# Expert weights against interleaved tokens: stationary blocks laid out in rows of 62 and 30 words

## Chip, cores and metric

The kernel runs on one core of one Trainium2 chip. The metric is the device time of one execution in microseconds. Everything is computed in float32 values. A float32 product is made from rounded parts (float32r): each operand is split into a high part and the low rest, and three matmuls of parts are summed.

## The reference, cut to what matters

Two layers of a streaming encoder run over 256 prompt tokens and 64 sample tokens, 1024 features wide. The change concerns the last stage alone, the top-2-of-8 SwiGLU experts of the second layer:

```python
def moe_ffn(x, w_r, wg, wu, wd):
    ...
    for e in range(N_EXPERTS):          # 8
        h = jax.nn.silu(xt @ wg[e]) * (xt @ wu[e])        # 1024 -> 3584
        y = y + gates[:, e:e + 1] * jnp.dot(h, wd[e])     # 3584 -> 1024
```

## The kernel before

The first 576 us compute both mixers and the dense feed-forward. What follows is the expert stage. Each expert works on a block of up to 128 tokens that were sent to it, gathered as rows into `xg`.

The weights of one expert come in 42 pieces (`NP`) of 128 x 2048 words, 336 pieces in all: 28 pieces of gate and up weights, 14 of down weights. SyncE loads a piece into one of seven slots of `raw` (L648). ScalarE rounds it into `split_hi` (`piece_hi`, L1207), and VectorE writes the rest, `raw - split_hi`, into `split_lo` (`piece_lo`, L1808). Both have three slots (`SR`), and ScalarE waits for TensorE to have used the piece three before.

On TensorE the weights are the moving operand, 512 columns at a time, and the tokens are the stationary one. A stationary operand is 128 partitions (features) by 128 columns (tokens), and each matmul loads its own. There are four sets of such blocks: `xgT_hi` and `xgT_lo` with 8 blocks each (the normalised input, transposed), and `hmT_hi` and `hmT_lo` with 28 blocks each (the gated hidden rows, transposed). For each piece TensorE issues 12 matmuls: high tokens and low tokens by high weights, then high tokens by low weights. They are L2475, L2479, L2484 for gate and up, L2510, L2513, L2519 for down, and L2495, L2496, L2502 for the last down piece:

```python
for c, o in enumerate(outs):
    TE.matmul(o, xgT_hi[:, kk, :], hi[:, w * k + 512 * c:w * k + 512 * c + 512], start=kk == 0, stop=False)
...
```

How the blocks are made: `hm` is transposed on TensorE by four transposes into one PSUM bank (L2528), in which the transposed tile is the stationary operand and takes every fourth word:

```python
last = TE.transpose(tb[n % 2][:, 128 * k:128 * k + 128], hm[:, m % 2, k:512:4], ident)
```

ScalarE copies the bank into `hmT_hi` with rounding (L1303), VectorE writes the rest to `hmT_lo` (L1952). This happens seven times for each expert. Near the end of an expert (piece `X_AT` = 39) the next expert's rows, which TensorE has transposed from `xg` by eight transposes (L1984), are scaled and written to `xgT_hi` by ScalarE (`xg_hi`, L1255) and to `xgT_lo` by VectorE (`xg_lo`, L1823).

At the very end the last expert's result is split into `last_y_hi` and `last_y_lo`, which lie in the places of `xgT_hi` and `xgT_lo`, and is sent back to its tokens by six matmuls for each of two halves (L2544 to L2552). In these every third one has a stationary operand of 64 columns.

The order of the work is written out by hand on each engine, and semaphores join the engines. Nothing of that order is changed.

Of the kernel before, what the change touches and what calls it, by code (L numbers as in the profile page):

```python
# [16 lines left out]
F32 = mybir.dt.float32  # L17
# [8 lines left out]
P = 128  # L26
D = 1024
# [221 lines left out]
def build(nc, A, O):  # L249
# [5 lines left out]
    with ExitStack() as ctx:  # L255
# [163 lines left out]
        hmT_hi = sb("hmT_hi", [P, FEB, P], FR)  # L419
# [38 lines left out]
        xgT_hi = sb("xgT_hi", [P, KB, P], FR)  # L458
        xgT_lo = sb("xgT_lo", [P, KB, P], FR)
# [5 lines left out]
        sb("below_hmT_lo", [P, 384])  # L465
        loop_only = ExitStack()
        hmT_lo = sb("hmT_lo", [P, FEB, P], FR, loop_only)
# [98 lines left out]
        last_y_hi = xgT_hi[:].rearrange("p k n -> p (k n)")  # L566
        last_y_lo = xgT_lo[:].rearrange("p k n -> p (k n)")
# [316 lines left out]
        def _(act):  # L884
# [364 lines left out]
            def xg_hi(base, first, ks=range(KB)):  # L1249

                for k in ks:
# [3 lines left out]
                    last = nc.scalar.activation(xgT_hi[:, k, :], b[:, 128 * (k % 4):128 * (k % 4) + 128], ACT.Copy, scale=gcol(3)[:, k:k + 1])  # L1255
# [18 lines left out]
            def experts(count, ip, done):  # L1274

                for i in range(done, count * NP):
# [51 lines left out]
        def _(dve):  # L1328
# [488 lines left out]
            def xg_lo(first, base, ks=range(KB)):  # L1817

                for k in ks:
                    if k % 4 == 0:  # L1820
                        dve.wait_ge(th_ready, base + (first + k // 4 + 1))
                    b = tb[(first + k // 4) % 2]
                    last = V.scalar_tensor_tensor(out=xgT_lo[:, k, :], in0=b[:, 128 * (k % 4):128 * (k % 4) + 128], scalar=gcol(3)[:, k:k + 1],  # L1823
                                                  in1=xgT_hi[:, k, :].bitcast(F32), op0=ALU.mult, op1=ALU.subtract)
# [103 lines left out]
            def experts(count, ip, done):  # L1928

                for i in range(done, count * NP):  # L1930
# [17 lines left out]
                    if q in HT_AT:  # L1948
# [3 lines left out]
                        V.tensor_tensor(hmT_lo[:, 4 * j:4 * j + 4, :].rearrange("p b n -> p (b n)"), tb[n % 2][:],  # L1952
                                        hmT_hi[:, 4 * j:4 * j + 4, :].rearrange("p b n -> p (b n)").bitcast(F32), ALU.subtract).then_inc(t_free, 1)
# [22 lines left out]
        def _(pe):  # L1976
# [462 lines left out]
            def experts(count, ip, first=False):  # L2439

                for i in range(count * NP):
# [27 lines left out]
                    if j < 2 * FC:  # L2469
                        n, w = 4 // len(ms), 512 * len(ms)  # L2470
                        outs = [banks[2 * up + (FC * h + m) % 2][:] for m in ms]
                        for k in range(n):
                            kk = n * s + k
                            for c, o in enumerate(outs):
                                TE.matmul(o, xgT_hi[:, kk, :], hi[:, w * k + 512 * c:w * k + 512 * c + 512], start=kk == 0, stop=False)  # L2475
                            if first and i == 0:
                                continue
                            for c, o in enumerate(outs):
                                TE.matmul(o, xgT_lo[:, kk, :], hi[:, w * k + 512 * c:w * k + 512 * c + 512], start=False, stop=False)  # L2479
                        pe.wait_ge(lo_ready, ip * (2 * NP) + (i + 1 + PR))  # L2480
                        for k in range(n):
                            kk = n * s + k
                            for c, o in enumerate(outs):
                                last = TE.matmul(o, xgT_hi[:, kk, :], lo[:, w * k + 512 * c:w * k + 512 * c + 512], start=False, stop=kk == KB - 1)  # L2484
# [122 lines left out]
```

## Time and profile before

| | us |
|---|---|
| median of 3 runs | 1537.97 |
| lowest and highest run | 1537.42, 1539.92 |
| span of the profiled execution, first to last instruction | 1535.8 |
| TensorE matmul busy | 1527.8 |
| TensorE weight load busy | 1333.0 |
| VectorE busy | 1234.4 |
| ScalarE busy | 998.9 |
| GpSimd busy | 217.5 |

The profiled execution has no time of its own beside its span, so sums are made on the span. The weight load is a queue of its own beside the matmuls and overlaps them. The record of a matmul is longer than its distance to the next one, since matmuls are pipelined: 390 ns long at a distance of 227 ns. The distance of their starts is what a matmul costs; in the merged timeline it is found from the starts of two lines and the counts between them.

### The profile page before, as it was taken

To read this page: it belongs to the slowest core of one execution; us is meant where nothing else is said; L and a number is where in the kernel's file an instruction comes from. 1 tells how busy PE (TensorE), PEld (TensorE's weight loads), DVE (VectorE), ACT (ScalarE), POOL (GpSimd) and SP (SyncE) were. 2 spreads that over 40 slices of the span, in tenths; PEclk is the share of its full clock that TensorE was granted. 3 is DMA by queue.
4 is the path that set the end of the run, shared out by engine and by line. 5 is a ranking of instruction groups with operands and counts; after the bars stand their busy time and mean duration, and the time that the engine had idled before them with its cause. 6 is when DMAs were issued, how large, how long until landed. Compare 5 with 4: busy or idle time off the path is not lost.

```text
span 1535.8 us, 21611 instructions
## 1 busy us (share of the span) xinstructions
PE 1527.8 (99%) x8428; PEld 1333.0 (87%) x8428; DVE 1234.4 (80%) x1253; ACT 998.9 (65%) x1079; POOL 217.5 (14%) x249
## 2 busy tenths in 40 slices
PE   9999999999999999999999999999999999999998
PEld 7989999999998988888888888888888888888887
DVE  5877666654477758988988888998998988898897
ACT  5655433333466547777777778777777777777775
POOL 5514400001150403101001001002002002002000
PEclk9999999999999999999999999999999999999999
DMA  8333455444443459999999999999999999999994
GB/s 226 96 110 116 149 164 164 133 157 151 125 122 110 141 209 367 383 366 388 372 381 376 374 374 376 391 359 386 384 363 382 381 362 379 400 361 363 394 373 183
DMA packets 159701, 437.43 MB, mean 285 GB/s; under 512 B 12068, under 2 KB 66176, under 8 KB 145264
## 3 DMA queue, kind: packets, MB, share of 16 engines
q1 hardware_dynamic: 151796, 423.02, 75.0%
q0 software_dynamic: 5552, 9.62, 2.3%
q10 hardware_dynamic: 2252, 3.41, 0.7%
q8 instruction: 68, 1.11, 0.3%
q14 instruction: 33, 0.27, 0.1%
HBM read 429.40 MB, written 13.60 MB: 288 GB/s over the span
## 4 chain that ended last, share of the span: by engine, by line
PE 98%; DMA 0%; ACT 0%; DVE 0%; issue 0%; SPq 0%; DVEq 0%; ACTq 0%
PE bank L1981 34%; PE bank L2475 13%; PE bank L2484 13%; PE bank L2479 13%; PE bank L2510 6%; PE bank L2513 6%; PE bank L2519 6%; PE bank L1984 3%; PE bank L2528 2%; PE bank L2496 0%; PE bank L2502 0%; PE bank L2495 0%; DMA gla<-b_g 0%; DVE x L1972 0%; ACT L1076 0%
## 5 line engine op out<-in xcount | busy, mean ns | idle before, releaser
L1808 DVE TENSOR_TENSOR split_lo<-raw,split_hi 128x2048 fp32r<-128x2048 f32 x336 | 763.1, 2289 | 101.8 <-ACT split_hi L1207 100.8
L1207 ACT CAST split_hi<-raw 128x2048 fp32r<-128x2048 f32 x336 | 640.5, 1911 | 224.5 <-PE bank L2484 145.7
L2475 PE MATMUL bank<-split_hi,xgT_hi 128*128 128x512 f32 x896 | 291.7, 395 | 0.0
L2479 PE MATMUL bank<-split_hi,xgT_lo 128*128 128x512 f32 x892 | 285.8, 390 | 0.0
L2484 PE MATMUL bank<-split_lo,xgT_hi 128*128 128x512 f32 x896 | 239.9, 390 | 0.0
L913 ACT CAST cut_hi<-ring 128x1024 fp32r<-128x1024 f32 x124 | 129.9, 1048 | 166.6 <-PE bank L1981 166.6
L1981 PE MATMUL bank<-xT_hi,cut_hi 128*128 128x320 f32 x752 | 236.7, 315 | 0.0
L1981 PE MATMUL bank<-xT_hi,cut_lo 128*128 128x320 f32 x752 | 233.5, 310 | 0.0
L1981 PE MATMUL bank<-xT_lo,cut_hi 128*128 128x320 f32 x752 | 231.9, 308 | 0.0
L1346 DVE TENSOR_TENSOR cut_lo<-ring,cut_hi 128x1024 fp32r<-128x1024 f32 x124 | 153.0, 1235 | 80.7 <-ACT cut_hi L913 79.9
L2484 PEld LDWEIGHTS bank<-split_lo,xgT_hi 128*128 128x128 f32 x896 | 168.3, 188 | 34.9
L2479 PEld LDWEIGHTS bank<-split_hi,xgT_lo 128*128 128x128 f32 x892 | 167.7, 188 | 34.7
L2475 PEld LDWEIGHTS bank<-split_hi,xgT_hi 128*128 128x128 f32 x896 | 166.2, 189 | 32.3
L1981 PEld LDWEIGHTS bank<-xT_hi,cut_hi 128*128 128x128 f32 x752 | 142.1, 189 | 1.6
L1981 PEld LDWEIGHTS bank<-xT_lo,cut_hi 128*128 128x128 f32 x752 | 142.2, 189 | 0.0
L1981 PEld LDWEIGHTS bank<-xT_hi,cut_lo 128*128 128x128 f32 x752 | 142.0, 189 | 0.0
L2510 PE MATMUL bank<-split_hi,hmT_hi 128*128 128x512 f32 x416 | 129.8, 393 | 0.0
L2513 PE MATMUL bank<-split_hi,hmT_lo 128*128 128x512 f32 x416 | 128.3, 390 | 0.0
L2519 PE MATMUL bank<-split_lo,hmT_hi 128*128 128x512 f32 x416 | 111.3, 390 | 0.0
L853 POOL COPY idc<-idx 128x1 uint32 (+1 forms) x8 | 5.7, 707 | 635.9 <-PE bank L1984 616.0
L2513 PEld LDWEIGHTS bank<-split_hi,hmT_lo 128*128 128x128 f32 x416 | 78.2, 188 | 16.3
L2519 PEld LDWEIGHTS bank<-split_lo,hmT_hi 128*128 128x128 f32 x416 | 78.1, 188 | 16.2
(316 smaller groups left out, 1723.2 us busy)
## 6 DMA issues: line engine op xcount, KB each, us to landing
raw<-moe_w_gate SPq DMA_DIRECT2D x112, 1024.0 KB, 7.8
raw<-moe_w_up SPq DMA_DIRECT2D x112, 1024.0 KB, 7.6
raw<-moe_w_down SPq DMA_DIRECT2D x112, 1024.0 KB, 7.3
ring<-w_in SPq DMA_DIRECT2D x15, 1024.0 KB, 5.5
ring<-ffn_w_gate SPq DMA_DIRECT2D x11, 1024.0 KB, 5.5
ring<-ffn_w_up SPq DMA_DIRECT2D x11, 1024.0 KB, 5.4
ring<-ffn_w_down SPq DMA_DIRECT2D x10, 1024.0 KB, 5.1
ring<-w_out SPq DMA_DIRECT2D x8, 1024.0 KB, 5.0
```

Source lines behind the costliest of these rows:

```text
L913: nc.scalar.copy(split_cut(cut_hi, q), raw_cut(q)).then_inc(cut_hi_ready, 1)
L1207: return nc.scalar.copy(split_hi[:, i % SR, :], raw_piece(i)).then_inc(hi_ready, 1)
L1346: V.tensor_tensor(split_cut(cut_lo, q), raw_cut(q), split_cut(cut_hi, q).bitcast(F32), ALU.subtract).then_inc(cut_lo_ready, 1)
L1808: V.tensor_tensor(split_lo[:, i % SR, :], raw_piece(i), split_hi[:, i % SR, :].bitcast(F32), ALU.subtract).then_inc(lo_ready, 1)
L1981: return TE.matmul(out, lhsT, rhs, start=start, stop=stop)
L1984: return TE.transpose(out, in_, ident[0:rows, 0:rows])
L2475: TE.matmul(o, xgT_hi[:, kk, :], hi[:, w * k + 512 * c:w * k + 512 * c + 512], start=kk == 0, stop=False)
L2479: TE.matmul(o, xgT_lo[:, kk, :], hi[:, w * k + 512 * c:w * k + 512 * c + 512], start=False, stop=False)
L2484: last = TE.matmul(o, xgT_hi[:, kk, :], lo[:, w * k + 512 * c:w * k + 512 * c + 512], start=False, stop=kk == KB - 1)
L2510: TE.matmul(banks[6 + n][:], hmT_hi[:, b, :], hi[:, c], start=b == 0, stop=False)
L2513: TE.matmul(banks[6 + n][:], hmT_lo[:, b, :], hi[:, c], start=False, stop=False)
L2519: last = TE.matmul(banks[6 + n][:], hmT_hi[:, b, :], lo[:, c], start=False, stop=b == FEB - 1)
```

## The change

The 128 words of one stationary block no longer lie side by side. In the new tile `spread` each token has a row of 62 words: words 0 to 7 are `xgT_hi`, 8 to 15 `xgT_lo`, 16 to 43 `hmT_lo`, and the rest is unused. In `spread_hi` each token has a row of 30 words, of which 28 are `hmT_hi`. So the consecutive columns of a stationary operand lie 248 or 120 bytes apart. The writes of ScalarE and VectorE go to the same places, one word every 248 or 120 bytes, and VectorE reads `hmT_hi` and `xgT_hi` back so. `last_y` gets a contiguous tile of its own where `xgT_hi` and `xgT_lo` were. Small pads place the two tiles 128 bytes further on than they would be without them; the tiles that lie above `spread_hi` move by 1,280 bytes, and `spread` by 1,152.

```diff
-        hmT_hi = sb("hmT_hi", [P, FEB, P], FR)
+        sb("below_spread_hi", [P, 32])
+        spread_hi = sb("spread_hi", [P, P, 30], FR)
+        sb("above_spread_hi", [P, 32])
...
-        xgT_hi = sb("xgT_hi", [P, KB, P], FR)
-        xgT_lo = sb("xgT_lo", [P, KB, P], FR)
+        last_y = sb("last_y", [P, 2, D], FR)
...
-        sb("below_hmT_lo", [P, 384])
+        sb("below_spread", [P, 352])
         loop_only = ExitStack()
-        hmT_lo = sb("hmT_lo", [P, FEB, P], FR, loop_only)
+        spread = sb("spread", [P, P, 62], FR, loop_only)
...
+        last_y_hi, last_y_lo = last_y[:, 0], last_y[:, 1]
+
+        def xgT_hi(k):
+            return spread[:, :, 0 + k]
+
+        def xgT_lo(k):
+            return spread[:, :, 8 + k]
+
+        def hmT_hi(b):
+            return spread_hi[:, :, 0 + b]
+
+        def hmT_lo(b):
+            return spread[:, :, 16 + b]
+
+        HMT_HI, HMT_LO = (spread_hi, 0), (spread, 16)
+
+        def four(part, j):
+            tile, first = part
+            return tile[:, :, first + 4 * j:first + 4 * j + 4].rearrange("p n s -> p s n")
+
+        def four_in(bank):
+            return bank[:].rearrange("p (s n) -> p s n", s=4)
...
-                    last = nc.scalar.activation(xgT_hi[:, k, :], b[:, 128 * (k % 4):128 * (k % 4) + 128], ACT.Copy, scale=gcol(3)[:, k:k + 1])
+                    last = nc.scalar.activation(xgT_hi(k), b[:, 128 * (k % 4):128 * (k % 4) + 128], ACT.Copy, scale=gcol(3)[:, k:k + 1])
...
-                        nc.scalar.copy(hmT_hi[:, 4 * j:4 * j + 4, :].rearrange("p b n -> p (b n)"), tb[n % 2][:]).then_inc(th_ready, 1)
+                        nc.scalar.copy(four(HMT_HI, j), four_in(tb[n % 2])).then_inc(th_ready, 1)
...
-                        V.tensor_tensor(hmT_lo[:, 4 * j:4 * j + 4, :].rearrange("p b n -> p (b n)"), tb[n % 2][:],
-                                        hmT_hi[:, 4 * j:4 * j + 4, :].rearrange("p b n -> p (b n)").bitcast(F32), ALU.subtract).then_inc(t_free, 1)
+                        V.tensor_tensor(four(HMT_LO, j), four_in(tb[n % 2]), four(HMT_HI, j).bitcast(F32), ALU.subtract).then_inc(t_free, 1)
...
-                                TE.matmul(o, xgT_hi[:, kk, :], hi[:, w * k + 512 * c:w * k + 512 * c + 512], start=kk == 0, stop=False)
+                                TE.matmul(o, xgT_hi(kk), hi[:, w * k + 512 * c:w * k + 512 * c + 512], start=kk == 0, stop=False)
```

The other matmuls of the stage and `xg_lo` change in the same way.

## Rows read from the trace of the kernel before

**Rows 1.** The page: span, rate of transfers in 40 slices, chain that ended last.
```profile
span 1535.8 us, 21611 instructions
...
GB/s 226 96 110 116 149 164 164 133 157 151 125 122 110 141 209 367 383 366 388 372 381 376 374 374 376 391 359 386 384 363 382 381 362 379 400 361 363 394 373 183
...
PE bank L1981 34%; PE bank L2475 13%; PE bank L2484 13%; PE bank L2479 13%; PE bank L2510 6%; PE bank L2513 6%; PE bank L2519 6%; PE bank L1984 3%; PE bank L2528 2%; PE bank L2496 0%; PE bank L2502 0%; PE bank L2495 0%; DMA gla<-b_g 0%; DVE x L1972 0%; ACT L1076 0%
```

**Rows 2.** Views of xgT_hi and hmT_hi: min/median/max ns, first and last start.
```profile
L2475 PE MATMUL bank<-split_hi,xgT_hi x896: 387/390/508, 576.5 to 1486.8; 128*128 128x512 f32 x180
...
L2510 PE MATMUL bank<-split_hi,hmT_hi x416: 388/390/477, 657.0 to 1523.3; 128*128 128x512 f32 x139
...
L2495 PE MATMUL bank<-split_hi,hmT_hi x32: 388/390/390, 693.8 to 1526.7; 128*128 128x512 f32 x32
...
L2502 PE MATMUL bank<-split_lo,hmT_hi x32: 389/390/390, 694.7 to 1527.4; 128*128 128x512 f32 x32
```

**Rows 3.** Timeline of TensorE at the tail: start us, us, instructions merged.
```profile
1527.65 0.85 PE L2544 MATMUL bank<-xgT_hi,last_hot 128*128 128x512 f32 x3
1528.33 0.84 PE L2548 MATMUL bank<-xgT_lo,last_hot 128*128 128x512 f32 x3
1529.01 0.86 PE L2544 MATMUL bank<-xgT_hi,last_hot 128*128 128x512 f32 x3
```

**Rows 4.** One stretch: length, PE, PEld, DVE, ACT, POOL busy, clock, DMA.
```profile
700.00:800.00 100.00, 100.00 (x459) 83.45 (x458) 89.06 (x50) 75.39 (x50) 5.39 (x4) 1.00 1.01 382
```

**Rows 5.** Timeline of TensorE around four transposes of hm.
```profile
720.10 1.07 PE L2484 MATMUL bank<-split_lo,xgT_hi 128*128 128x512 f32 x4
...
722.82 1.08 PE L2484 MATMUL bank<-split_lo,xgT_hi 128*128 128x512 f32 x4
723.74 0.63 PE L2528 MATMUL bank<-const_sb,hm 128*128 128x128 f32 x4
...
724.67 0.62 PE L2479 MATMUL bank<-split_hi,xgT_lo 128*128 128x512 f32 x2
```

**Rows 6.** Timeline of TensorE around eight transposes of xg.
```profile
678.41 1.07 PE L2519 MATMUL bank<-split_lo,hmT_hi 128*128 128x512 f32 x4
679.32 1.03 PE L1984 MATMUL bank<-const_sb,xg 128*128 128x128 f32 x8
...
680.66 0.62 PE L2513 MATMUL bank<-split_hi,hmT_lo 128*128 128x512 f32 x2
```

**Rows 7.** Weight loads (tile views: min/median/max ns; by line: busy us, mean ns).
```profile
L2544 PEld LDWEIGHTS bank<-xgT_hi,last_hot x6: 134/188/188, 1527.4 to 1529.2; 128*128 128x128 f32 x4, 128*64 128x64 f32 x2
...
L2528 PEld LDWEIGHTS bank<-const_sb,hm 128*128 128x128 f32 x224 | 35.6, 204 | 4.5 <-DVE hm L1946 0.5
...
L1984 PEld LDWEIGHTS bank<-const_sb,xg 128*128 128x128 f32 x64 | 7.5, 140 | 1.0
...
L2528 PE MATMUL bank<-const_sb,hm x224: 270/283/386, 604.7 to 1499.4; 128*128 128x128 f32 x112
```

**Rows 8.** VectorE's splits of 2048 and 1024 elements: busy us, mean ns, idle before.
```profile
L1808 DVE TENSOR_TENSOR split_lo<-raw,split_hi 128x2048 fp32r<-128x2048 f32 x336 | 763.1, 2289 | 101.8 <-ACT split_hi L1207 100.8
...
L1346 DVE TENSOR_TENSOR cut_lo<-ring,cut_hi 128x1024 fp32r<-128x1024 f32 x124 | 153.0, 1235 | 80.7 <-ACT cut_hi L913 79.9
```

**Rows 9.** Timeline of VectorE at the end of the first expert.
```profile
687.33 2.15 DVE L1823 SCALAR_TENSOR_TENSOR xgT_lo<-bank,pcol,xgT_hi 128x128 fp32r<-128x128 f32 x8
689.40 8.90 DVE L1808 TENSOR_TENSOR split_lo<-raw,split_hi 128x2048 fp32r<-128x2048 f32 x4
```

**Rows 10.** Timeline of TensorE: sixteen fp32 matmuls with eight stationary columns.
```profile
560.77 4.47 PE L1981 MATMUL bank<-xR,wr 128*8 128x320 f32 x16
```

**Rows 11.** The same by line from 559 to 566 us: busy us, mean ns.
```profile
L1981 PE MATMUL bank<-xR,wr 128*8 128x320 f32 x16 | 4.5, 433 | 0.0
```

**Rows 12.** Timeline of TensorE in the dense feed-forward, 18 matmuls apart.
```profile
400.06 0.31 PE L1981 MATMUL bank<-hT_hi,cut_hi 128*128 128x320 f32 x1
...
402.70 0.31 PE L1981 MATMUL bank<-hT_hi,cut_hi 128*128 128x320 f32 x1
```

More of the change, by code:

```diff
@@ L1822, in xg_lo @@
                     b = tb[(first + k // 4) % 2]
-                    last = V.scalar_tensor_tensor(out=xgT_lo[:, k, :], in0=b[:, 128 * (k % 4):128 * (k % 4) + 128], scalar=gcol(3)[:, k:k + 1],
-                                                  in1=xgT_hi[:, k, :].bitcast(F32), op0=ALU.mult, op1=ALU.subtract)
+                    last = V.scalar_tensor_tensor(out=xgT_lo(k), in0=b[:, 128 * (k % 4):128 * (k % 4) + 128], scalar=gcol(3)[:, k:k + 1],
+                                                  in1=xgT_hi(k).bitcast(F32), op0=ALU.mult, op1=ALU.subtract)
                     if k % 4 == 3:
@@ L2478, in experts @@
                             for c, o in enumerate(outs):
-                                TE.matmul(o, xgT_lo[:, kk, :], hi[:, w * k + 512 * c:w * k + 512 * c + 512], start=False, stop=False)
+                                TE.matmul(o, xgT_lo(kk), hi[:, w * k + 512 * c:w * k + 512 * c + 512], start=False, stop=False)
                         pe.wait_ge(lo_ready, ip * (2 * NP) + (i + 1 + PR))
@@ L2483, in experts @@
                             for c, o in enumerate(outs):
-                                last = TE.matmul(o, xgT_hi[:, kk, :], lo[:, w * k + 512 * c:w * k + 512 * c + 512], start=False, stop=kk == KB - 1)
+                                last = TE.matmul(o, xgT_hi(kk), lo[:, w * k + 512 * c:w * k + 512 * c + 512], start=False, stop=kk == KB - 1)
                         if first and i == 0:
@@ L2488, in experts @@
                                 for c, o in enumerate(outs):
-                                    last = TE.matmul(o, xgT_lo[:, k, :], hi[:, w * k + 512 * c:w * k + 512 * c + 512], start=False, stop=False)
+                                    last = TE.matmul(o, xgT_lo(k), hi[:, w * k + 512 * c:w * k + 512 * c + 512], start=False, stop=False)
                     elif q == NP - 1:
@@ L2494, in experts @@
                                 c = slice(1024 * k + 512 * n, 1024 * k + 512 * n + 512)
-                                TE.matmul(banks[6 + n][:], hmT_hi[:, b, :], hi[:, c], start=False, stop=False)
-                                TE.matmul(banks[6 + n][:], hmT_lo[:, b, :], hi[:, c], start=False, stop=False)
+                                TE.matmul(banks[6 + n][:], hmT_hi(b), hi[:, c], start=False, stop=False)
+                                TE.matmul(banks[6 + n][:], hmT_lo(b), hi[:, c], start=False, stop=False)
                             if n == 0:
@@ L2501, in experts @@
                                 c = slice(1024 * k + 512 * n, 1024 * k + 512 * n + 512)
-                                last = TE.matmul(banks[6 + n][:], hmT_hi[:, b, :], lo[:, c], start=False, stop=k == 1)
+                                last = TE.matmul(banks[6 + n][:], hmT_hi(b), lo[:, c], start=False, stop=k == 1)
                             if n == 0:
@@ L2518, in experts @@
                                 c = slice(1024 * k + 512 * n, 1024 * k + 512 * n + 512)
-                                last = TE.matmul(banks[6 + n][:], hmT_hi[:, b, :], lo[:, c], start=False, stop=b == FEB - 1)
+                                last = TE.matmul(banks[6 + n][:], hmT_hi(b), lo[:, c], start=False, stop=b == FEB - 1)
                     last.then_inc(piece_used, 1)
```

6 lines of the change are left out of this document (2 added, 4 removed).

## Prediction

> **What bounds the kernel now.** I read the page first. Its span is 1535.8 us [rows 1]; the median of the runs shown, 1537.97 us, lies 2.2 us above it, and I add those 2.2 us to every sum made on this execution. The experts' matmuls run from 576.5 us [rows 2] to 1527.65 us [rows 3], 951 us. Inside it TensorE is busy for all of a 100 us window while VectorE is at 89% and ScalarE at 75% [rows 4]. The chain that ended last goes through TensorE's lines only: L2475, L2484 and L2479 with 13% each, L2510 and L2513 with 6% each [rows 1]. So the question is what one expert matmul costs TensorE from start to start, not how long its record is.
>
> The timeline gives that. Between the starts of the last four matmuls of one piece and of the next piece, 720.10 and 722.82, lie 12 matmuls: 2.72 us, 0.2267 us each [rows 5]. At 2.4 GHz (granted clock 1.00 [rows 4]) 512 columns take 0.2133, so 13.4 ns per matmul are not columns. The count is 896 on L2475, 416 on L2510, 32 on L2495 [rows 2], each with two companions: 4032 matmuls, 914 us. The rest are transposes. From 722.82 to 724.67 stand six such matmuls and four transposes of `hm`: 1.85 less 1.36 is 0.49 us for four [rows 5]; from 678.41 to 680.66 six matmuls and eight transposes of `xg`: 2.25 less 1.36 is 0.89 for eight [rows 6]. With 56 fours and 8 eights that is 914 + 27 + 7 = 948 of the 951 us. There is no stall to win back; the stage is 4032 cadences.
>
> **What the change moves.** (a) No instruction is added or removed. Every one of the 4032 stationary operands, until now 128 consecutive words, becomes 128 words that lie 248 or 120 bytes apart. (b) ScalarE and VectorE write these words, and VectorE reads the high ones back, at the same distance. (c) Tiles above lie 1,280 or so bytes further on.
>
> **(a) on the path.** A load of weights runs beside the matmul before it. For contiguous fp32r weights it takes 188 ns with 128 columns and 134 with 64 [rows 7]: 0.84 ns a column on top of 80 ns. The 0.84 × 128 = 108 ns of columns have a cadence of 227 ns to hide in. What does distance cost? The trace has one distant stationary: `hm[:, m % 2, k:512:4]`, one word in 16 bytes. Its load takes 204 ns, that of the contiguous `xg` in the same kind of transpose 140 [rows 7]. Less the 80 ns, 0.97 against 0.47 ns a column: twice as slow. Transposes of `xg` cost 0.89/8 = 0.111 us each, those of `hm` 0.49/4 = 0.122, so where the load is the limit the distance shows.
>
> It matters here only if the load outgrows 227 ns, or disturbs the stream of the matmul beside it. For the first: if a distant column costs 0.97 ns in an fp32r load too, the load is 80 + 0.97 × 128 = 204 ns long, with 124 ns of columns: hidden. For the second: the first `hm` load of a group runs beside an fp32r matmul. The last four matmuls before `hm` start at 722.82, and the first `hm` transpose at 723.74: 0.92 us [rows 5]; before `xg` 678.41 to 679.32, 0.91 [rows 6]. One resolution step apart, so a distant load beside a 512-column stream costs at most 0.01 us in this one place, and the nearest row gives nothing. I take nothing for (a): the cover is the 213 ns stream, and the price without it is in the first rival. Ends kept: a gain of 11 ns and a loss of 17 ns per matmul, from the rivals.
>
> [...]
>
> **(b) off the path.** VectorE takes (2289 - 1235)/1024 = 1.03 ns an element [rows 8]; I use it for ScalarE too. No row writes at such a distance; below nothing I see no reason for a gain, above I allow a doubling, as for the load. Then each `hmT` copy grows by 512 elements, 0.53 us, seven times an expert, and the eight `xgT` pieces by 1.05 us together, on either engine. VectorE gets 4.8 us more in an expert's 118.6 us (948.5/8) and goes from 89% to 93%: no bound. The tightest place is the end of an expert. There the eight `xgT` low parts take 2.15 us and four piece splits follow without a break, 8.90 us; the second ends at 693.85 [rows 9], and the matmul that reads it, the first of L2502, starts at 694.7 [rows 2]: 0.85 us to spare. I take nothing for (b); with both doublings 2.1 us would arrive there, 1.25 beyond the cover.
>
> **(c)** The same 0.2267 holds over `xgT` and `hmT` and all three slots of the split tiles, so I price placement at nothing. `last_y` stays contiguous, and the tail is unchanged. The DMA queue moves the same bytes.
>
> Sum: 1535.8 + 0 + 0 + 0, and 2.2: 1538.0 us. Its own range is 1535 to 1541.
>
> **Rivals.** *A load that pays twice (slower).* A contiguous fp32r load takes 0.84 ns a column where the transpose's takes 0.47. If that is because it goes over its columns twice, a distant column costs 2 × 0.97 = 1.94 ns, and 248 ns of columns no longer fit under 227. Twice the cadence of load-bound `hm` transposes is 2 × 0.122 = 0.244 us; taken from inside a group, (0.63 - 0.283)/3 = 0.116 [rows 5], where 0.283 is the length of one record [rows 7], it is 0.231. The cost is 4032 × 5 to 17 ns, 20 to 70 us; in the middle 45, 1583 us. It decides as soon as a column costs above 227/128 = 1.77 ns. [...] Chance 0.20. [...]
>
> *The 13.4 ns are a collision between the load's reads and the stream's, and the new distance avoids it (faster).* An fp32 matmul of 320 columns beside a load of eight columns has a cadence of (4.47 - 0.43)/15 = 0.269 us [rows 10, 11], two passes of 133.3 ns and only 2.7 ns over. So without a full load beside it a matmul can follow at 2 to 3 ns. The full prize is 11 ns × 4032 = 44 us: 1494 us. VectorE's 2.51 us a piece (89% of 948.5/336) fits under the 2.69 that would be left, and the transfers would have to go from 382 [rows 4] to about 400 GB/s, where single slices show 400 [rows 1]. Against it: 18 matmuls of 320 columns take 402.70 - 400.06 = 2.64 us, 0.1467 each, 13.4 ns over 133.3 [rows 12]: the excess does not grow with the stream. At the tail every third load has 64 columns instead of 128, and six matmuls take 1.36 us, 0.2267 each [rows 3], no less than elsewhere as far as rows of 10 ns can tell: it doesn't shrink with the load either. A fixed cost per switch would not care about layout. But all of these loads are contiguous; the trace has no fp32r matmul beside a distant fp32r load, and 13 ns could be the part of many collisions that any contiguous walk has. It pays from 0.8 ns a matmul. Chance 0.33.
>
> *Distant writes that come late (slower, small).* As worked out under (b): 1.25 us at eight places, 10 us, 1548. It decides once both engines' additions exceed 0.85 us. Nothing shows the price of such writes. Chance 0.10.
>
> **How the numbers follow.** Forecast 0.37, the three rivals 0.33, 0.20 and 0.10. The prediction is the likeliest case, 1538 us. A change under 0.2% (3 us) can't be told from none here. Faster is the collision case, 0.33; same 0.37; slower 0.20 + 0.10 = 0.30. As cases of both signs hold most of the chance, the range has to reach both full prices: from 1493 to 1585 us; more than the middle of the slow case is the part left out.
>
> **What would show it.** If I am right, in the profile after the loads of L2475 to L2519 have a mean of about 204 ns instead of 188, and a piece still takes 2.72 us. The twice-paying load shows a load record near 330 ns and a piece of 2.8 to 2.9 us. The collision shows a piece near 2.6 us, with load records of any length. Late writes show as ScalarE's and VectorE's `spread` rows growing, and a gap in front of L2502. I am wrong above all if an fp32r load reads otherwise than a transpose's does, since the one distant load of this trace is a transpose's.

## The result, and the profile after

| | before | after |
|---|---|---|
| median (lowest to highest), us | 1537.93 (1537.42 to 1539.92), 4 runs | 1619.31 (1617.7 to 1620.85), 4 runs |
| ratio, 95% interval | | 1.0532, 1.0517 to 1.0547 |
| span of the profiled execution, us | 1535.8 | 1619.1 |

The change costs 81.4 us. That is 5.3%, on the slow side and beyond the range that ended at 1585. Divided by the 4032 matmuls it is 20.2 ns each.

The page of the changed kernel answers to [rows 1]: the span, the busy times, the rate of transfers and the chain.
```profile
span 1619.1 us, 21611 instructions
...
PE 1610.3 (99%) x8428; PEld 1572.8 (97%) x8428; DVE 1274.7 (79%) x1253; ACT 1033.8 (64%) x1079; POOL 216.9 (13%) x249
...
GB/s 215 93 129 124 153 157 150 145 161 131 118 136 91 170 344 359 337 353 351 343 338 363 342 331 371 341 330 368 342 345 360 336 335 362 344 344 333 364 337 164
...
PE 98%; DMA 0%; ACT 0%; DVE 0%; issue 0%; SPq 0%; DVEq 0%; ACTq 0%
```
The number of instructions is the same. A slice is now 40.5 us long instead of 38.4, so the expert stage begins in the 15th; from the 16th slice on each one moves less per second than before. The time went into the expert stage, and TensorE is still the whole chain. What is new is the weight load (PEld): it was busy for 1333.0 of 1535.8 us, and is now for 1572.8 of 1619.1.

The weight loads by line and shape, changed kernel (busy us, mean ns, idle before); [rows 7] had 188 ns for a load of this shape:
```profile
L2499 PEld LDWEIGHTS bank<-split_hi,spread 128*128 128x128 f32 x892 | 264.0, 334 | 0.0
L2495 PEld LDWEIGHTS bank<-split_hi,spread 128*128 128x128 f32 x896 | 263.9, 332 | 0.1
...
L2539 PEld LDWEIGHTS bank<-split_lo,spread_hi 128*128 128x128 f32 x416 | 112.4, 335 | 0.0
L2548 PEld LDWEIGHTS bank<-const_sb,hm 128*128 128x128 f32 x224 | 35.8, 204 | 0.9
```
"Distant" means here and below that neighbouring words of a block don't lie side by side. In these rows the distant fp32r loads take 332 to 335 ns (328 to 335 over all lines of the stage), and the queue has next to no idle time before them. The distant transposes of `hm`, which the change does not touch, still take 204.

Busy time of each engine, granted clock and transfers between 700 and 800 us of the changed kernel, as in [rows 4]:
```profile
700.00:800.00 100.00, 100.00 (x418) 99.91 (x418) 86.79 (x48) 73.64 (x49) 4.88 (x3) 1.00 0.97 352
```
The clock is still 1.00, so it is not the clock. VectorE went from 89.06 to 86.79 although its writes grew: it now works for a slower TensorE, with 48 operations in the window instead of 50. The loads fill 99.91 of 100 us, and 418 instead of 459 matmuls fit.

The timeline of TensorE in the changed kernel, around one group of transposes and at the same place of two pieces four apart, as in [rows 5]:
```profile
736.42 1.14 PE L2504 MATMUL bank<-split_lo,spread 128*128 128x512 f32 x4
737.40 0.63 PE L2548 MATMUL bank<-const_sb,hm 128*128 128x128 f32 x4
737.79 0.84 PE L2495 MATMUL bank<-split_hi,spread 128*128 128x512 f32 x2
738.47 0.66 PE L2499 MATMUL bank<-split_hi,spread 128*128 128x512 f32 x2
...
747.41 0.65 PE L2495 MATMUL bank<-split_hi,spread 128*128 128x512 f32 x2
...
759.20 0.65 PE L2495 MATMUL bank<-split_hi,spread 128*128 128x512 f32 x2
```
From 747.41 to 759.20 are 48 matmuls, 0.2456 us each, where it was 0.2267. That is 18.9 ns, and 4032 of them are 76.2 us. From 736.42 to 738.47 are six matmuls and four transposes: 2.05 us, less 6 × 0.2456 leaves 0.576 for the four, where 0.49 was left. The first two matmuls behind the transposes take 0.68 us, where two take 0.49 elsewhere. The likely reason is that the load behind the last short transpose has no 213 ns stream to hide under. (The 213 ns are 512 columns at 0.4167 ns: 512 columns take 0.2267 us [rows 5] and 320 take 0.1467 [rows 12], 0.0800 us for 192 more. The prediction's 2.4 GHz comes to the same 0.4167.) 56 × 0.086 is 4.8 us. The two together are 81.0 of the 81.4 us: carried over to the whole stage, these distances account for the loss.

The copies into the distant tiles, changed kernel (min/median/max ns, first and last start):
```profile
L1324 ACT CAST spread_hi<-bank x56: 1159/1177/1197, 614.0 to 1585.3; 128x512 fp32r<-128x512 f32 x56
L1973 DVE TENSOR_TENSOR spread<-bank,spread_hi x56: 1150/1208/1251, 616.3 to 1587.6; 128x512 fp32r<-128x512 f32 x56
```
In the kernel before these two took 577 and 684 ns (medians of L1303 and L1952). ScalarE's copy doubled (2.04 times), VectorE's took 1.77 times as long. The prediction had allowed 0.53 us more for each; they are 0.60 and 0.52.

VectorE at the end of the first expert in the changed kernel, as in [rows 9]:
```profile
697.57 3.06 DVE L1844 SCALAR_TENSOR_TENSOR spread<-bank,pcol,spread 128x128 fp32r<-128x128 f32 x8
700.53 8.98 DVE L1829 TENSOR_TENSOR split_lo<-raw,split_hi 128x2048 fp32r<-128x2048 f32 x4
...
705.98 0.65 PE L2522 MATMUL bank<-split_lo,spread_hi 128*128 128x512 f32 x2
```
The last line is TensorE's, from its timeline. The eight low parts take 3.06 instead of 2.15 us. The second split behind them ends near 705.0 (700.53 + half of 8.98), and its reader starts at 705.98. Nothing waits here: the cover is 0.95 us, where it was 0.85.

### The profile page after: what moved, and what is told of

Same layout as the page of the kernel before. It is cut to its first block, busy times and chain, and to the rows that moved or that the text cites. A ratio compares the mean times of both kernels' runs of the same rounds, so it can differ in the third digit from the quotient of the medians.

```text
span 1619.1 us, 21611 instructions
## 1 busy us (share of the span) xinstructions
PE 1610.3 (99%) x8428; PEld 1572.8 (97%) x8428; DVE 1274.7 (79%) x1253; ACT 1033.8 (64%) x1079; POOL 216.9 (13%) x249
## 4 chain that ended last, share of the span: by engine, by line
PE 98%; DMA 0%; ACT 0%; DVE 0%; issue 0%; SPq 0%; DVEq 0%; ACTq 0%
PE bank L2001 32%; PE bank L2495 14%; PE bank L2504 14%; PE bank L2499 14%; PE bank L2530 6%; PE bank L2539 6%; PE bank L2533 6%; PE bank L2004 3%; PE bank L2548 2%; PE bank L2516 0%; PE bank L2522 0%; PE bank L2515 0%; DMA gla<-b_g 0%; DVE x L1992 0%; ACT L1097 0%
## 5 line engine op out<-in xcount | busy, mean ns | idle before, releaser
L2495 PE MATMUL bank<-split_hi,spread 128*128 128x512 f32 x896 | 311.8, 418 | 0.0
L2499 PE MATMUL bank<-split_hi,spread 128*128 128x512 f32 x892 | 302.1, 408 | 0.0
L2495 PEld LDWEIGHTS bank<-split_hi,spread 128*128 128x128 f32 x896 | 263.9, 332 | 0.1
L2499 PEld LDWEIGHTS bank<-split_hi,spread 128*128 128x128 f32 x892 | 264.0, 334 | 0.0
L2504 PE MATMUL bank<-split_lo,spread 128*128 128x512 f32 x896 | 256.9, 409 | 0.0
L2504 PEld LDWEIGHTS bank<-split_lo,spread 128*128 128x128 f32 x896 | 239.8, 334 | 0.0
L2001 PE MATMUL bank<-xT_hi,cut_hi 128*128 128x320 f32 x752 | 236.5, 314 | 0.0
L2530 PE MATMUL bank<-split_hi,spread_hi 128*128 128x512 f32 x416 | 139.4, 416 | 0.0
L2533 PE MATMUL bank<-split_hi,spread 128*128 128x512 f32 x416 | 136.2, 409 | 0.0
L2530 PEld LDWEIGHTS bank<-split_hi,spread_hi 128*128 128x128 f32 x416 | 121.0, 335 | 0.0
L2539 PE MATMUL bank<-split_lo,spread_hi 128*128 128x512 f32 x416 | 120.2, 411 | 0.0
L2533 PEld LDWEIGHTS bank<-split_hi,spread 128*128 128x128 f32 x416 | 119.5, 330 | 0.0
L2539 PEld LDWEIGHTS bank<-split_lo,spread_hi 128*128 128x128 f32 x416 | 112.4, 335 | 0.0
```

Source lines behind the costliest of these rows:

```text
L2001: return TE.matmul(out, lhsT, rhs, start=start, stop=stop)
L2495: TE.matmul(o, xgT_hi(kk), hi[:, w * k + 512 * c:w * k + 512 * c + 512], start=kk == 0, stop=False)
L2499: TE.matmul(o, xgT_lo(kk), hi[:, w * k + 512 * c:w * k + 512 * c + 512], start=False, stop=False)
L2504: last = TE.matmul(o, xgT_hi(kk), lo[:, w * k + 512 * c:w * k + 512 * c + 512], start=False, stop=kk == KB - 1)
L2530: TE.matmul(banks[6 + n][:], hmT_hi(b), hi[:, c], start=b == 0, stop=False)
L2533: TE.matmul(banks[6 + n][:], hmT_lo(b), hi[:, c], start=False, stop=False)
```

## The experiments

All ratios are against the kernel before. "Cadence" is the distance of two starts of the timeline divided by the matmuls between them, in gate and up pieces past 1000 us where not said otherwise. The theories at the start, by the letters that the expectations use: the load reads a distant word at about twice the price and no longer fits under the stream (L); a distant load slows the stream beside it (S); the distant writes come late or get in TensorE's way (W). A fourth is the place of the tiles.

### Writes and reads apart

**Distant writes, contiguous reads.** All of the changed kernel's writes stay. TensorE reads one contiguous block instead, a copy of the identity:
```diff
+        still = sb("still", [P, P], FR)
...
+            V.tensor_copy(still[:], ident).then_inc(still_ready, 1)
...
-                                TE.matmul(o, xgT_hi(kk), hi[:, w * k + 512 * c:w * k + 512 * c + 512], start=kk == 0, stop=False)
+                                TE.matmul(o, still[:], hi[:, w * k + 512 * c:w * k + 512 * c + 512], start=kk == 0, stop=False)
```


> The changed kernel, but all 4032 expert matmuls take one contiguous stationary block of 128 words (the identity) instead of the distant ones, so the experts' products are left out; ScalarE and VectorE still write and read back every distant word. Theory L (the weight load itself reads distant words at about 1.95 ns a column and sets the cadence): loads back at 188 ns, a piece 2.72 us, 1538 to 1542 us. Theory S (a distant load disturbs the stream beside it): the same. Theory W (ScalarE's and VectorE's distant accesses come late or compete with TensorE's reads): the 81 us stay, about 1619 us.

Measured: 1544.72 us against 1536.07, ratio 1.0054 (1.0037 to 1.0071). The loads, a stretch of the stage, and the timeline at its start in this kernel:
```profile
L2507 PEld LDWEIGHTS bank<-split_lo,still 128*128 128x128 f32 x896 | 168.7, 188 | 35.3
```
```profile
578.15 2.08 PE L2498 MATMUL bank<-split_hi,still 128*128 128x512 f32 x4 [3.35 <-DVE still L1899]
...
583.34 0.62 PE L2498 MATMUL bank<-split_hi,still 128*128 128x512 f32 x2
...
1000.26 1.07 PE L2507 MATMUL bank<-split_lo,still 128*128 128x512 f32 x4
...
1011.14 1.07 PE L2507 MATMUL bank<-split_lo,still 128*128 128x512 f32 x4
```
```profile
578.00:583.00 5.00, 4.85 (x11) 3.80 (x12) 3.58 (x28) 1.49 (x2) 2.14 (x3) 0.50 1.02 365
```
The loads are back at 188 ns and the cadence at 10.88/48 = 0.2267 us. What is left over is mostly the experiment's own. TensorE waits 3.35 us for the copy of the identity and starts the stage at 578.15 us instead of 576.46. The twelve matmuls that follow run at a granted clock of 0.50: (583.34 - 578.15)/12 is 0.4325 us instead of 0.2267, 2.5 us in all. An expert lasts 119.0 us instead of 118.73, which is 2.2 us over eight. These three are 6.4 of the 6.5 us between the two spans, and only the 2.2 can be charged to distant writes. W falls as the cause of the 81 us.

The 2.2 us are real, though, and lie where the prediction looked for them. The loads of the last low parts of an expert, VectorE's timeline before them, and TensorE's at that place:
```profile
L2525 PEld LDWEIGHTS bank<-split_lo,still 128*128 128x128 f32 x32 | 5.4, 188 | 3.5 <-DVE split_lo L1831 2.8
```
```profile
694.79 8.90 DVE L1831 TENSOR_TENSOR split_lo<-raw,split_hi 128x2048 fp32r<-128x2048 f32 x4
```
```profile
699.01 0.39 PE L2519 MATMUL bank<-split_hi,still 128*128 128x512 f32 x1
699.34 0.73 PE L2525 MATMUL bank<-split_lo,still 128*128 128x512 f32 x2
```
The second of the four splits ends near 694.79 + 4.45 = 699.24, and its reader starts at 699.34, 0.33 us behind the matmul before it instead of 0.227. The cover of 0.85 us is used up, and TensorE waits there once in each of the eight experts.

**Distant reads, contiguous writes.** The kernel before, except that every matmul of the stage reads one block at 120 bytes a column:
```diff
+        still = sb("still", [P, P, 30], FR)
...
+            V.tensor_copy(still[:, :, 0], ident).then_inc(still_ready, 1)
...
-                                TE.matmul(o, xgT_hi[:, kk, :], hi[:, w * k + 512 * c:w * k + 512 * c + 512], start=kk == 0, stop=False)
+                                TE.matmul(o, still[:, :, 0], hi[:, w * k + 512 * c:w * k + 512 * c + 512], start=kk == 0, stop=False)
```


> The kernel before, with all its writes contiguous, but all 4032 expert matmuls take one stationary block whose 128 words lie 120 bytes apart (the identity), so the experts' products are left out. L and S: load records near 332 ns, a piece 2.96 us, 1615 to 1622 us. W: 1538 us. Together with the distant writes alone the two differences should add up to the 81 us.

Measured: 1636.18 us, ratio 1.0645 (1.0627 to 1.0663). One of its rows of loads, and the start and end of three pieces of its timeline:
```profile
L2487 PEld LDWEIGHTS bank<-split_lo,still 128*128 128x128 f32 x896 | 243.5, 339 | 0.4
```
```profile
1011.08 1.16 PE L2487 MATMUL bank<-split_lo,still 128*128 128x512 f32 x4
...
1020.06 1.16 PE L2487 MATMUL bank<-split_lo,still 128*128 128x512 f32 x4
```
Reads alone give the loss, and more: the cadence is 8.98/36 = 0.2494 us, not 0.2456, and the 100 us exceed the 81. Some 5.7 us are the late start, as above (the stage begins at 580.59 us, and its first eight matmuls, at a mean granted clock of 0.52, take (584.18 - 580.59)/8 = 0.449 us each), 91.5 are the cadence, which leaves some 3 for the transposes. So the 1615 to 1622 us that were expected, and the two differences adding up to 81, did not come. In this kernel every block lies at 120 bytes, and all matmuls read the same one; at 120 bytes alone the series below has 0.2475 us. The other 2 ns are not explained.

### Is the load the limit?

**Fewer moving columns.** The changed kernel with 384 of the 512 moving columns in all but the first matmul of a sum:
```diff
-                                TE.matmul(o, xgT_lo(kk), hi[:, w * k + 512 * c:w * k + 512 * c + 512], start=False, stop=False)
+                                TE.matmul(o[:, 0:N], xgT_lo(kk), hi[:, w * k + 512 * c:w * k + 512 * c + N], start=False, stop=False)
```


> The changed kernel with 384 instead of 512 moving columns in every expert matmul but the first of each sum; a quarter of the experts' outputs is left out. L: the load needs its 247 ns however short the stream is, so the cadence stays at 0.247 us and the time within 3 us of 1619. S: the stream costs 160 + 13 + 20 = 193 ns, TensorE is no longer the bound, VectorE's work of some 113 us an expert is, about 1490 us.

Measured: 1613.63 us, ratio 1.0497 (1.0479 to 1.0514). Five pieces of its timeline:
```profile
1001.93 1.15 PE L2505 MATMUL bank<-split_lo,spread 128*128 128x384 f32 x4
...
1016.66 1.14 PE L2505 MATMUL bank<-split_lo,spread 128*128 128x384 f32 x4
```
14.73/60 is 0.2455 us. A quarter of the stream is gone, 128 × 0.4167 = 53 ns a matmul, and the cadence is the same as far as rows of 10 ns tell. In the changed kernel the load is the limit, not the stream. S, which expected 0.193 us, falls as the cause of the loss. The time is 5.7 us below the changed kernel's, a little outside the 3 us that L allowed: over a whole expert it is 128.29 us instead of 128.99, or 1.4 ns for each of 504 matmuls. So the shorter stream gives back a little, but not more.

**Fewer stationary columns.** The changed kernel with 96 of 128 stationary columns in nearly all matmuls:
```diff
-                                TE.matmul(o, xgT_lo(kk), hi[:, w * k + 512 * c:w * k + 512 * c + 512], start=False, stop=False)
+                                TE.matmul(o[0:M_], xgT_lo(kk)[:, 0:M_], hi[:, w * k + 512 * c:w * k + 512 * c + 512], start=False, stop=False)
```


> The changed kernel with 96 instead of 128 stationary columns in every expert matmul but the first and last of each sum; 32 of an expert's tokens are left out of most sums. L: the load's columns take 96 x 1.97 = 189 ns (record 270) and hide under 227, so the cadence is 0.227 again, except for about 32 of 504 matmuls: 1541 to 1547 us. S: three quarters of the 20 ns stay, about 1599 us. It also tells whether the cost has a threshold or grows with every column.

Measured: 1571.76 us, ratio 1.0226 (1.0209 to 1.0244). A row of its loads, and two pieces of its timeline in which every load has 96 columns:
```profile
L2500 PEld LDWEIGHTS bank<-split_hi,spread 128*96 128x96 f32 x892 | 222.4, 260 | 0.0
```
```profile
1009.11 1.10 PE L2505 MATMUL bank<-split_lo,spread 128*96 128x512 f32 x4
...
1014.72 1.09 PE L2505 MATMUL bank<-split_lo,spread 128*96 128x512 f32 x4
```
The load gets 74 ns shorter for 32 columns. Its 260 - 80 = 180 ns of columns now fit under the stream, but the cadence is 5.61/24 = 0.2338 us and not 0.2267. Neither expected time came, 1541 to 1547 (L) or 1599 (S). So there is a second cost, 7.1 ns here, that remains when the load is hidden, and L has only the first of the two.

### The price against the distance

Here only `xgT` changes, 2688 of the 4032 matmuls (L2475, L2479, L2484), in the kernel before; `hmT` stays contiguous and serves as a control. One token's row is of r words. For 2, 3, 4 and 16 words the 16 blocks lie in groups of r, for the others in one:
```diff
-        xgT_hi = sb("xgT_hi", [P, KB, P], FR)
-        xgT_lo = sb("xgT_lo", [P, KB, P], FR)
+        xrows = sb("xrows", [P, 4, P, 4], FR)
...
+        def xgT_hi(k):
+            return xrows[:, k // 4, :, k % 4]
```
8 bytes, rows of 2 words:

> [...] If any distance other than one word costs the full price: 332 ns and 1592 us.

12 bytes, rows of 3 words:

> [...] By full price for any distance: 1592.

16 bytes, rows of 4 words, where the changed kernel has the far distances of 120 and 248 bytes:

> [...] If the far distance has a price of its own (banks): less than 1592.

64 bytes, rows of 16 words:

> The same with rows of 16 words: columns 64 bytes apart, in the same 8 KB of the tile as before. [...] If banks that repeat every 64 or 128 bytes matter: clearly more than at 16 bytes.

128 bytes, rows of 32 words:

> The kernel before with only xgT_hi and xgT_lo (2688 matmuls) in rows of 32 words, columns 128 bytes apart. [...] Theory B (memory banks repeat every 128 bytes, and a load whose next column falls into the same bank waits for it; 120 and 248 bytes are 8 short of such a period, so every second step stays in the bank): every step stays in the bank, record well over 339 ns, cadence over 0.250 us.

72 bytes, rows of 18 words:

> [...] Theory B: no step stays in the bank, record 302 to 312 ns, cadence 0.236.

120 bytes, rows of 30 words:

> The kernel before with only xgT_hi and xgT_lo (2688 matmuls) in rows of 30 words, 120 bytes apart, as spread_hi has them. Theory C (the distance of 120 bytes itself makes the load slow): record 333 to 340 ns, cadence 0.246 to 0.250 us, an expert of about 125.5 us. Theory D (placement, or that every block is distant, made it slow): record 302 to 312, cadence 0.236, as at 16, 64, 72 and 128 bytes.

124 bytes, rows of 31 words:

> The same in rows of 31 words, 124 bytes apart, 4 short of 128. If the load gets slow the nearer the distance comes to 128 bytes from below: record at least 335 ns. If 120 bytes is special by itself: 302 to 312.

136 bytes, rows of 34 words:

> The same in rows of 34 words, 136 bytes apart, 8 over 128. If it is the sign that counts, a walk that falls behind the 128-byte period while the stream runs forward: record 302 to 312 ns. If it is the two steps within one 16-byte column of the period, forward or back: about 335 ns.

| distance, bytes | us (before) | ratio, interval | load record, ns | cadence, ns |
|---|---|---|---|---|
| 8 | 1553.83 (1535.99) | 1.0115, 1.0098 to 1.0132 | 193 | 233.3 |
| 12 | 1561.80 (1535.99) | 1.0169, 1.0152 to 1.0186 | 253 | 235.5 |
| 16 | 1564.00 (1535.99) | 1.0186, 1.0169 to 1.0203 | 312 | 236.7 |
| 64 | 1566.18 (1535.99) | 1.0199, 1.0182 to 1.0216 | 302 | 236.5 |
| 72 | 1564.49 (1537.3) | one run | 306 | 235.6 |
| 128 | 1570.27 (1537.3) | one run | 305 | 237.4 |
| 120 | 1598.20 (1535.29) | one run | 334 | 247.5 |
| 124 | 1574.38 (1535.29) | one run | 315 | 239.6 |
| 136 | 1594.78 (1535.29) | one run | 332 | 246.7 |

A row of loads of the kernel with 8 bytes, and its control:
```profile
L2490 PEld LDWEIGHTS bank<-split_lo,xrows 128*128 128x128 f32 x896 | 173.3, 193 | 36.1
...
L2519 PEld LDWEIGHTS bank<-split_hi,hmT_lo 128*128 128x128 f32 x416 | 78.1, 188 | 16.4
```
Five pieces of the timeline at 8 bytes (14.00/60 = 0.2333):
```profile
999.78 1.09 PE L2490 MATMUL bank<-split_lo,xrows 128*128 128x512 f32 x4
...
1013.78 1.10 PE L2490 MATMUL bank<-split_lo,xrows 128*128 128x512 f32 x4
```
A row of loads of the kernel with 16 bytes:
```profile
L2485 PEld LDWEIGHTS bank<-split_hi,xrows 128*128 128x128 f32 x892 | 249.7, 312 | 0.0
```
And with 120, with two pieces of its timeline (5.94/24 = 0.2475):
```profile
L2485 PEld LDWEIGHTS bank<-split_hi,xrows 128*128 128x128 f32 x892 | 265.2, 334 | 0.0
```
```profile
1000.02 1.15 PE L2490 MATMUL bank<-split_lo,xrows 128*128 128x512 f32 x4
...
1005.96 1.16 PE L2490 MATMUL bank<-split_lo,xrows 128*128 128x512 f32 x4
```
The record grows in three steps, 193, 253 and 312 ns at 8, 12 and 16 bytes, and does not grow further at 64, 72 and 128 bytes. The steps are 60 and 59 ns. An estimate from these records: counted by the stretches of 16 bytes that the 128 columns touch, 64, 96 and 128 of them, it is 1.86 ns for each on top of 74, and the count stays 128 at 64, 72 and 128 bytes, where the records are 302, 306 and 305. Contiguous columns touch 32 and take 188, not the 134 that this would give, so for them the estimate does not hold; what lies behind it no run shows. The full price for any distance other than one word (332 ns, 1592 us) did not come: 8 bytes have 193 ns and 1553.83 us, 12 have 253 and 1561.80. 16 and 64 bytes stayed far below 1592 us as well, with 1564.00 and 1566.18, and 64 bytes were not dearer in the load than 16. At 8 bytes the load is only 5 ns longer than a contiguous one, and the kernel still 17.8 us slower.

Distances of 8 bytes less or more than 128 take a fourth step, to 334 and 332, and so does 248, 8 less than twice 128, in the changed kernel (L2499). 124 bytes lie between, at 315. It is not a matter of multiples of 16 bytes: 72 is none and takes 306. Theory B, memory banks that repeat every 128 bytes, fell with 128 itself, which takes 305 where well over 339 was expected; no run shows such banks or such a period. What stands (C) is that 120 bytes are dear with nothing else changed, 334 ns and 247.5, and so are 136, 332 and 246.7. Why is open, and for these distances there is one run each.

In all these kernels the contiguous `hmT` loads beside them kept the record of 188 ns, and the starts of their matmuls the median distance of 227 ns.

### The place of the tiles

The changed kernel with both tiles 128 bytes lower:
```diff
-        sb("below_spread_hi", [P, 32])
...
-        sb("above_spread_hi", [P, 32])
+        sb("above_spread_hi", [P, 64])
...
-        sb("below_spread", [P, 352])
+        sb("below_spread", [P, 320])
```


> The changed kernel with the two tiles 128 bytes lower and everything else where it was. If only the distance between columns counts: 1619 us, a piece of 2.96 us, load records 332 ns, all as in the changed kernel. If where the tiles lie against the split tiles counts: the cadence moves by more than 2 ns, over 8 us.

Measured: 1620.41 us against 1537.3, ratio 1.0538 (1.0522 to 1.0554), within the interval of the change itself. The six main rows of loads have 332 to 334 ns as in the changed kernel. At this other place nothing differs, and the 120 bytes were as dear in the two kernels above that have other tiles around them. Placement falls as a cause; no further places were tried.

### The second cost: distance and stream

The kernels with rows of 4, 2 and 1 words, each with 384 moving columns in gate and up pieces (not in the first matmul of a sum). Against those with 512 the edit is that of the experiment with fewer moving columns.

> Rows of 4 words again, with 384 instead of 512 moving columns in the gate and up matmuls except the first of each sum; a quarter of those outputs is left out. If at 16 bytes the load is the limit: the cadence stays at 0.236 us. If the 9 ns are a disturbance of the stream: it falls until the load binds, by record 312 less the 90 ns by which records of binding loads outlast the cadence, to 0.222 us.

> Rows of 2 words with 384 instead of 512 moving columns in the gate and up matmuls except the first of each sum; a quarter of those outputs is left out. Within a piece, if each load costs the stream a fixed 6 ns: 160 + 13 + 6 = 0.180 us. If the cost grows with the columns streamed: 0.178. If the load at 8 bytes binds after all: 0.233, unchanged.

> The control: contiguous columns as in the kernel before, with 384 moving columns in the same matmuls. Within a piece 160 + 13.4 = 0.173 us, record 188 ns; TensorE then waits for VectorE between pieces, so the time says little and the cadence inside a piece is what is read.

Measured, one run each: 1555.72 us (before 1535.29), 1475.62 and 1475.81 (before 1537.65). Three pieces of the timeline at 16 bytes:
```profile
1002.16 1.09 PE L2491 MATMUL bank<-split_lo,xrows 128*128 128x384 f32 x4
...
1010.57 1.09 PE L2491 MATMUL bank<-split_lo,xrows 128*128 128x384 f32 x4
```
One piece at 8 bytes, and the loads:
```profile
1023.23 0.86 PE L2491 MATMUL bank<-split_lo,xrows 128*128 128x384 f32 x4
...
1025.31 0.86 PE L2491 MATMUL bank<-split_lo,xrows 128*128 128x384 f32 x4
```
```profile
L2491 PEld LDWEIGHTS bank<-split_lo,xrows 128*128 128x128 f32 x896 | 158.2, 197 | 17.4 <-DVE split_lo L1815 13.4
```
One piece with contiguous blocks:
```profile
1023.63 0.85 PE L2491 MATMUL bank<-split_lo,xrows 128*128 128x384 f32 x4
...
1025.71 0.85 PE L2491 MATMUL bank<-split_lo,xrows 128*128 128x384 f32 x4
```
At 16 bytes the cadence is 8.41/36 = 0.2336 us although the stream is only 0.160: the load sets it, and 233.6/128 = 1.82 ns is what a column costs there. Beside 512 columns it was 0.2367, so there, too, the longer stream adds some 3 ns. At 8 bytes and contiguous it is 2.08/12 = 0.1733 us in both, to 10 ns in a piece. So the 6.6 ns that 8 bytes cost beside 512 columns are not there beside 384. None of the three expected values for 8 bytes (0.180, 0.178, 0.233) came. The second cost is real, since three kernels show it (8 bytes 6.6, 12 bytes 8.8, 96 stationary columns 7.1 ns), but it is not a fixed price of a distant load. That the load is hidden is measured for 8 bytes alone, by these 173 ns; for the other two it is inferred from their records, 253 and 260 ns. What the second cost depends on is open.

### The other way round

If distance makes loads dear, the one distant operand of the kernel before could be made contiguous: `hm` written so that its transposes read consecutive words.
```diff
-                            V.scalar_tensor_tensor(out=hm[:, m % 2, :], in0=banks[2 + m % 2][:], scalar=now_w[:, h % 2, 0:1], in1=hs[:, m % 2, :],
+                            V.scalar_tensor_tensor(out=hm[:, m % 2, :].rearrange("p (k n) -> p n k", k=4), in0=banks[2 + m % 2][:].rearrange("p (n k) -> p n k", k=4), scalar=now_w[:, h % 2, 0:1], in1=hs[:, m % 2, :].rearrange("p (n k) -> p n k", k=4),
...
-                            last = TE.transpose(tb[n % 2][:, 128 * k:128 * k + 128], hm[:, m % 2, k:512:4], ident)
+                            last = TE.transpose(tb[n % 2][:, 128 * k:128 * k + 128], hm[:, m % 2, 128 * k:128 * k + 128], ident)
```


> The kernel before with its one distant stationary removed: VectorE writes hm so that each of the four transposes reads 128 contiguous words (it writes 512 bytes apart instead). If a distant load costs a transpose 0.122 against 0.111 us, 224 of them give back 2.5 us, about 0.16%; VectorE's 56 products grow from 0.74 to at most 1.27 us, 3.7 us an expert, which its idle share covers. Load records of the transposes 204 to 140 ns. If the writes come late instead: no gain or a loss.

Measured: 1543.36 us against 1537.3, ratio 1.0046 (1.0032 to 1.006), a loss of 0.5% that is small but clear of its interval. Its write of `hm`, the load of its transposes, and its timeline at the first group of an expert:
```profile
L1946 DVE SCALAR_TENSOR_TENSOR hm<-bank,now_w,hs 128x512 f32<-128x512 f32 x56 | 59.9, 1140 | 0.0
...
L2528 PEld LDWEIGHTS bank<-const_sb,hm 128*128 128x128 f32 x224 | 26.0, 141 | 15.1 <-DVE hm L1946 8.2 <-issue 2.6
```
```profile
1006.92 1.07 PE L2484 MATMUL bank<-split_lo,xgT_hi 128*128 128x512 f32 x4
1008.00 0.66 PE L2528 MATMUL bank<-const_sb,hm 128*128 128x128 f32 x4
1008.95 0.50 PE L2475 MATMUL bank<-split_hi,xgT_hi 128*128 128x512 f32 x1 [0.29 <-DVE hm L1946]
```
The load falls from 204 to 141 ns, as it should. But VectorE's write, now with 512 bytes between words, grows from 744 to 1140 ns, and TensorE waits for it: the transposes begin 1.08 us after the last four matmuls where 0.92 was usual [rows 5], and the next matmul is 0.29 us late behind them. By the starts in the trace these two places make 0.92 of the 0.99 us that an expert takes longer. The distance has only been moved to an engine whose output TensorE is waiting for. No version tried beats the kernel before.

## Why the prediction was wrong

**What bounds the kernel** was right: the stage is 4032 cadences, and 81.0 of the 81.4 us were found in cadences and at transposes.

**The step that failed** is in (a): "if a distant column costs 0.97 ns in an fp32r load too, the load is 80 + 0.97 × 128 = 204 ns long, with 124 ns of columns: hidden." The records were 332 to 335 ns, and the load set the cadence at 245.6 ns. By the same working a column costs (333 - 80)/128 = 1.98 ns, twice 0.97. The rival that named this mechanism, the load that pays twice, is the one that happened, with the record near 330 ns that it announced; a piece took 12 × 0.2456 = 2.95 us, a little over its 2.8 to 2.9. What the runs show is the factor: at 16 bytes, the one distance that both kinds of load have, a column takes (312 - 80)/128 = 1.81 ns against the transpose's 0.97, 1.87 times. That the load goes over its columns twice, the reason that the rival gave, is not shown by any run. The evidence was in hand. The only distant load of the trace was a transpose's, and [rows 7] already showed that a transpose's contiguous column (0.47) is not the fp32r load's (0.84). I took a price from one kind of load for the other and left the factor between them out for the distant case alone.

**The rival's size** was too small as well: 5 to 17 ns a matmul, 45 us in the middle. It was made from the cadence of `hm` transposes (0.231 to 0.244 us), which is that of 16 bytes. At 16 bytes 384 columns beside it give 0.2336, so for that distance it was right. But at 120 and 248 bytes a column costs more, 0.2455/128 = 1.92 ns. The rival's own price of a column, 1.94 ns, gave 248 ns of load and so 248 - 227 = 21 ns, 86 us; the measured cost is 20.2 ns. I had both figures, took the middle of the lower one and cut the range there. That 1.94 comes so near to 1.92 is partly luck. It was worked out for 16 bytes, where a column costs 1.82, and the dearer distances of 120 and 248 bytes, which nothing in the prediction foresaw, made up the difference. The 4.8 us at the loads behind the transposes were in no sum.

**A distant load beside the stream costs nothing** was the second error, and in another kernel it would have been the deciding one. I had a bound of 0.01 us from one resolution step (0.92 against 0.91 us) and took its lower end for 4032 matmuls. In three kernels with hidden loads it is 6.6 to 8.8 ns. Times 4032 that is 27 to 35 us. Beside 384 columns it is nothing, 173.3 ns at 8 bytes and contiguous; beside 512 it is 6.6 ns at 8 bytes, and where in TensorE it arises no run shows. In the changed kernel itself it hardly adds, since there the load is the limit: a quarter less stream changed an expert by 1.4 ns a matmul.

**The chance of that rival**, 0.20, was too low. The factor 0.84/0.47 stood in [rows 7], and no row spoke against it. Two things were in no part of the prediction: the stream beside a load is slowed at 8 bytes already (233.3 for 226.7 ns), and the loads at 120 and 136 bytes are dearer than at 128 (334 and 332 against 305 ns).

**(b), the writes**, was right for the changed kernel: they grew by about what was allowed and nothing waited for them. The rival "distant writes that come late" did not happen there, because the slower TensorE gave the cover back. With TensorE at its old pace (distant writes, contiguous reads) it did happen, in front of the reader of the late low parts as described, and cost 2.2 us in eight experts instead of the 10 that both full doublings would have.

**(c), placement**, was right as far as it was tried: 128 bytes lower changed nothing.

**The collision rival (faster, 0.33)** was wrong. The argument against it in the prediction held and is now shown at a third length: contiguous blocks beside 384 columns have 173.3 - 160 = 13.3 ns over the stream at 0.4167 ns a column, as beside 512 (226.7 - 213.3) and 320 (146.7 - 133.3). It is the same excess for each matmul at all three lengths, and no layout tried took it away. What it is made of stays open. The 2.7 ns of the fp32 matmul came from taking it as two passes. The rows show that its columns cost about twice as much, (269 - 111)/192 = 0.82 ns between 128 and 320 of them [rows 6, 10, 11]; passes no run shows. The rival was given almost the chance of the forecast on the ground that no row excluded it.

## What to carry to other kernels

In these runs a load of weights on TensorE set the cadence where its columns, the record less 80 ns, took longer than the cadence beside contiguous blocks: 245.6 ns for 226.7 at 120 and 248 bytes, and 233.6 for 173.3 at 16 bytes beside 384 columns. Even a shorter one was not always free: 6.6 ns at 8 bytes beside 512 columns. Before the layout of a stationary operand is changed, work out its load with the price of its own kind of load, data type and distance, and compare it with the cadence: here 128 columns had 227 ns, that is 1.77 ns a column, and the distant layout asks 1.92. Where a trace has the distant case for one kind of load only, carry over the ratio between the kinds and not the figure. And if words must lie apart somewhere, the question is which of writer and reader has the slack; here neither the load nor the write of `hm` had it.

## What was not expected of the hardware

- An fp32r load of 128 columns takes 188 ns contiguous, 193 at 8 bytes, 253 at 12, 302 to 312 at 16, 64, 72 and 128, 315 at 124, and 332 to 339 at 120, 136 and 248 bytes. A transpose's load takes 140 contiguous and 204 at 16 bytes.
- A load that sets the cadence has a record 87 to 98 ns longer than the cadence: 333 against 246 in the changed kernel, 343 against 245.5 in it beside 384 columns, 329 against 234 at 16 bytes beside 384. The 80 ns on top of the columns, taken from contiguous loads, were close to it.
- A distant load can slow a stream that hides it: by 6.6 ns at 8 bytes beside 512 columns, yet by nothing beside 384.
- ScalarE's and VectorE's writes of a 128 x 512 piece go from 577 and 684 ns to 1177 and 1208 with 120 and 248 bytes between words. For 128 x 128 pieces of `xgT` they are 376 and 343 contiguous, 388 and 345 at 8 bytes, 492 and 450 at 16, and 500 and 467 at 248: the writes, too, are nearly free at 8 bytes and dear from 16 on, with 439 and 393 at 12 between. VectorE reads the high part back at the same distance, so its figures hold for both together.
- After a wait of 3.35 us in front of the stage TensorE ran twelve matmuls at the granted clock 0.50, 0.4325 us each. This cost 2.5 us more than the wait.
